# Splitting 512 tokens in 258 and 254 columns in place of 264 and 248 in the seven-product pairs of a float32 decoder trunk

## The reference, cut to what matters

```
D_MODEL, SEQ, D_FF = 1024, 512, 2816
def swiglu(h, w_gate, w_up, w_down):
    return (jax.nn.silu(h @ w_gate) * (h @ w_up)) @ w_down

h = h + 0.5 * swiglu(rmsnorm(h, ffn1_norm[layer]), ffn1_w_gate[layer], ffn1_w_up[layer], ffn1_w_down[layer])
...
h = h + 0.5 * swiglu(rmsnorm(h, ffn2_norm[layer]), ffn2_w_gate[layer], ffn2_w_up[layer], ffn2_w_down[layer])
```

## Time and profile before

| what | value |
|---|---|
| median of 3 runs | 2118.63 us (2118.48 to 2120.15) |
| span of the profiled execution, first to last instruction | 2115.9 us |
| TensorE busy | 2105.4 us, 13030 matmuls |
| of these on L813 to L815 (seven-product pairs) | 5712, which is 68 pairs of 84 |
| VectorE, ScalarE, GpSimd busy | 1306.5, 812.3, 1552.4 us |
| mean granted TensorE clock | 0.999 |

### The profile page before, as it was taken

The page is one execution under the profiler, slowest core; times in us unless marked ns, Lnnn a source line. Parts: engine busy times, 40 slices in busy tenths (PEclk is TensorE's granted clock), DMA queues, the critical chain, the costliest instruction groups (busy, mean ns, idle before and its releaser), DMA issues. The chain is left out here.

```text
span 2115.9 us, 36325 instructions
## 1 busy us (share of the span) xinstructions
PE 2105.4 (100%) x13030; PEld 1856.4 (88%) x13030; DVE 1306.5 (62%) x1949; ACT 812.3 (38%) x1546; POOL 1552.4 (73%) x1390
## 2 busy tenths in 40 slices
PE   9999999999999999999999999999999999999998
PEld 7899988888888899998889998886878888999987
DVE  6876796695444576664376666456872546676533
ACT  5255312034223355541245552134362334555312
POOL 7778897667973778788778887785757557788864
PEclk9999999999999999999999999999999999999999
DMA  5333333223331333333233333332322212333332
GB/s 200 114 120 115 100 95 121 90 80 97 126 104 50 95 101 115 106 101 123 90 99 106 106 110 101 99 100 75 105 89 91 80 61 87 117 101 115 100 95 85
DMA packets 115417, 215.04 MB, mean 102 GB/s; under 512 B 12832, under 2 KB 14400, under 8 KB 115008
## 3 DMA queue, kind: packets, MB, share of 16 engines
q1 hardware_dynamic: 111024, 202.03, 29.9%
q10 hardware_dynamic: 4240, 10.99, 1.5%
HBM read 208.77 MB, written 4.19 MB: 101 GB/s over the span
## 5 line engine op out<-in xcount | busy, mean ns | idle before, releaser
L527 POOL TENSOR_TENSOR w_split<-w_raw,w_split 128x512 fp32r<-128x512 f32 (+1 forms) x486 | 670.3, 1379 | 41.4 <-ACT w_split L1801 1.1
L603 PE MATMUL ps<-x,w_split 128*128 128x512 f32 (+1 forms) x1766 | 682.1, 386 | 0.3 <-DVE tg L2197 0.2
L605 PE MATMUL ps<-x,w_split 128*128 128x512 f32 (+1 forms) x1766 | 674.1, 382 | 0.0
L604 PE MATMUL ps<-x,w_split 128*128 128x512 f32 (+1 forms) x1766 | 673.9, 382 | 0.0
L517 POOL TENSOR_SCALAR w_split<-w_raw 128x512 fp32r<-128x512 f32 x482 | 335.1, 695 | 351.6 <-PE ps L605 336.9
L813 PE MATMUL ps<-x,w_split 128*128 128x264 f32 (+1 forms) x1904 | 535.1, 281 | 1.1 <-DVE ps L2300 1.0
L815 PE MATMUL ps<-x,w_split 128*128 128x264 f32 (+1 forms) x1904 | 535.1, 281 | 0.0
L814 PE MATMUL ps<-x,w_split 128*128 128x264 f32 (+1 forms) x1904 | 533.5, 280 | 0.0
L603 PEld LDWEIGHTS ps<-x,w_split 128*128 128x128 f32 x1766 | 331.8, 188 | 74.0 <-issue 9.4
L605 PEld LDWEIGHTS ps<-x,w_split 128*128 128x128 f32 x1766 | 331.9, 188 | 64.9
L604 PEld LDWEIGHTS ps<-x,w_split 128*128 128x128 f32 x1766 | 332.0, 188 | 64.7 <-issue 1.4
(11 more groups left out here) (342 smaller groups left out, 2476.0 us busy)
## 6 DMA issues: line engine op xcount, KB each, us to landing
w_raw<-in_stream SPq DMA_DIRECT2D x758, 256.0 KB, 2.8
arena<-in_memT ACTq DMA_DIRECT2D x2, 1024.0 KB, 5.8
s_tables<-kv ACTq DMA_DIRECT2D x4, 512.0 KB, 3.0
arena<-s_tables ACTq DMA_DIRECT2D x4, 512.0 KB, 4.4
out<-h ACTq DMA_DIRECT2D x6, 256.0 KB, 2.3
h<-in_xT SPq DMA_DIRECT2D x4, 256.0 KB, 4.8
h<-in_xT SPq DMA_DIRECT2D x2, 512.0 KB, 6.1
w_raw<-in_stream SPq DMA_DIRECT2D x5, 128.0 KB, 5.0
```

The lines of the kernel that those rows point to most:

```text
L527: pool.tensor_tensor(lo, x, hi.bitcast(F32), ALU.subtract).then_inc(split_ready if half else S("half_split"), 1)
L603: pe.matmul(dst, wh, xh, start=start, stop=False)
L604: pe.matmul(dst, wh, xl, start=False, stop=False)
L605: return pe.matmul(dst, wl, xh, start=False, stop=stop)
```

## The change

One constant is changed. Everything that is worked out from it moves with it: the four wide products go from 264 to 258 columns, the three narrow ones from 248 to 254; the copies, joins and token sums change their widths in the same way; `LEAD` goes from 16 to 4; the narrow moving operands begin at column 258, byte 1032 of the row, in place of 264, byte 1056; and the product B11 is written from column 254 of its bank in place of 248.

```
-FIRST_T, SECOND_T = 264, 248
+FIRST_T, SECOND_T = 258, 254
 LEAD = FIRST_T - SECOND_T
```

## The result

The changed kernel takes 2127.03 us (median) against 2118.85 us for the kernel before: the ratio is 1.0031, with a 95% interval of 1.0020 to 1.0042. It is slower, by 8.2 us in the medians. One of the six runs of the changed kernel was disturbed (5424 us) and counts in neither. The profiled execution took 2127.03 us with a span of 2125.2 us, 9.3 us above the span of before. In all runs whose own span is on record the time is 1.8 to 2.5 us above it; the 2.7 us named ahead of the prediction set a median against the span of one execution. By an estimate from these figures that execution took 2117.7 to 2118.4 us, less than the median, so some of the 9.3 us is that, and not the change.

A forecast was written before the change was run, and what follows sets the result against it. TensorE, busy 2105.4 of 2115.9 us, was taken as the bound. Per pair -0.06 + 0.22 = +0.15 us after rounding, over 68 pairs +10.2 us, median 2118.6 to 2128.8 us; own range 2126 to 2134, 8-in-10 range 2112.5 to 2134.

The forecast's parts named there:

- Term 1: Four wide products of a pair, 48 matmuls of 258 in place of 264 columns: 5.76 against 5.82 us, a 0.06 us gain.
- Term 2: Three narrow products of a pair, 36 matmuls of 254 in place of 248 columns: 4.32 against 4.10 us, a 0.22 us loss.
- The 256 row: Profile row of 256-column matmuls, 95 starts in 11.39 us, 119.9 ns each; taken as the price of 254 and 258 columns.
- the forecast's own bounds: Whole change: +7.6 us with straight pieces through the 248, 256 and 264 rows; +15 us if 258 columns kept 121.3 ns.
- The staircase: TensorE's pitch is columns plus a fixed cost of 17 to 24 cycles, rounded up to 16; inferred from 248, 256, 264, 512.
- The straight line: Rival, chance 0.16: pitch grows evenly from 248 to 264 columns, 0.46 ns a column; -2.3 us, no change that shows.
- The lower step: Rival, chance 0.13: 254 columns still take 272 cycles, under 115 ns, while wide products settle at 119.9; -4.4 to -5.8 us.
- The signs that the prediction named beforehand: Changed pair's timeline: every product 1.44 us; T3 at 1.36, 1.39 to 1.40 or 1.52 shows a rival; wide 1.46 refutes.
- The start off the grid: Rival, chance 0.10: narrow operands from byte 1032, no multiple of 16, cost 6.7 ns more per matmul; +27 us, 2145.
- Parts 3 to 5: Joins and copies: 8 ns each at most, covered; token adds 29 ns, 0 to +0.5 us kept; no new TensorE wait.

The follow-up runs named there:

- the second: The changed kernel (258 and 254) run and profiled once more, unchanged, beside the split of 256: 1.0032 (1.0020 to 1.0045) of the kernel before.
- The streams of one width: Trunk left out; TensorE alone streams 48 matmuls for each width and start: from column 0, 254 columns 117.6 ns, 258 119.9, 260 118.7.
- the start at 256: Changed kernel, but TensorE reads the narrow operands from column 256 (byte 1024) in place of 258: 1.0026 (1.0016 to 1.0036) of the kernel before.

## Why the prediction was right, and where its sizes were off

*What bounds the kernel.* Right. TensorE has no new wait, and the even pairs with nothing beside them take the kernel's times.

*The time.* 2128.8 us was predicted, 2127.0 measured; +10.2 us against +8.2, from a pair of 10.07 against 10.02 and 10.05 us. By the even pairs alone it is +6.9 in that profile and +6.7 in the second; part of the nearness of 8.2 to 10.2 is therefore luck. The direction, and the reason for it, that the narrow products lose more than the wide ones win because 254 columns cost far more than 248, hold.

*Term 1, the wide products (48 x 119.9 ns = 5.76 us, a gain of 0.06 us).* They take 5.78 and 5.79 us (2.88 + 1.46 + 1.44, and 2.89 + 1.44 + 1.46), 120.4 and 120.6 ns: a gain of 0.03 to 0.04 us. A stream of 258 has my 119.9; behind narrow products it does not hold it.

*Term 2, the narrow products (36 x 119.9 ns = 4.32 us, a loss of 0.22 us).* This is the term that was mis-sized. They take 4.24 and 4.26 us, 117.8 and 118.3 ns: a loss of 0.14 to 0.16 us. The 256 row was the nearest row and stood for one product of three. The two errors partly cancel, which is why the sum is nearer than its terms. The lower of the forecast's own bounds, straight pieces through the rows of 248, 256 and 264 columns, would have been the better figure: 118.4 and 120.2 ns, a pair of 10.03 us, +7.6 us. The streams of one width give no reason for it, though, since there 260 columns cost less than 258.

*The staircase.* As a rule it fell. It was inferred from four widths; 18 widths and other starts show no grid of 16 cycles (116.7, 117.6, 118.7, 122.3 ns). One of its four supports was not in the rows either: 264 columns outside the pairs had 120.6 ns, which is 289.4 cycles and not 288. Where it was used, at 254 and 258, it said 120 for both; 258 alone has that, 254 alone has 116.7. The even 120 ns and the uneven 264 that I read as a fixed cost near 24 are patterns of a stream, not places on a step. The Trainium skill's line ("TensorE: Matmul & The Clock Gate", Back-to-back issue gap), which the page gives for isolated matmuls, comes to 108.3 ns at 254 columns, and the trace disagrees there too.

*The rivals.* The straight line is refuted by the falling pitches, though for 254 alone its 116.7 ns happens to be the measured one. The lower step is refuted: no stream of 254 is under 116.7 ns, and its limit was 115. The signs that the prediction named beforehand would have misled: T3 at 1.40 us in the first and third block is the straight line's figure, not the forecast's 1.44, and of the wide products B22 is at 1.46, the figure that was to refute the first term. A single product told less than the sum of the seven. The start off the grid is refuted by the stream and by the start at 256. The line rule on 16 bytes ("SBUF — State Buffer", Specifications, in the Trainium skill) does not order what was measured: 254 columns touch 64 lines from each of the three starts tried, and byte 1032 is the cheapest; 248 columns touch 63 lines from columns 258 and 262, and these are the cheapest and the dearest of four starts (113.5 and 117.4 ns).

*Parts 3 to 5.* Joins 8 ns, token adds 25 ns where 29 was worked out, 0.2 us more of waits in the pairs: as predicted.

*What stays open.* What inside TensorE makes the patterns is not settled: a weight load and a moving stream share each pitch, but no run separates them. Nor is it shown what picks 10.05 in place of 10.02.

## What to carry to other kernels

Where TensorE is a plain stream with a weight load for every matmul and some 250 columns, take the price of a width from a stream of whole groups in their own order, alone on the core: it gave the kernel's pair to the nanosecond in most blocks, and within 0.03 us where the kernel took up another pattern (10.05 at 258), while prices of single widths (268: 120.0 ns alone, 124.4 in the pair) and of one part of a change at a time did not add up. Sweep such a width in steps of two before settling it: here 260 and 252 beat 264 and 248 by 0.12% and 258 and 254 by 0.4% with no other edit. The nearest row gave the direction here and missed the narrow pitch by 1.8% (119.9 against 117.8 ns); by the same row 260 and 252 would have been slower too (10.08 us a pair), and they are faster (9.87).

## What the runs showed of the hardware that was not expected

The pitch of three-part float32 matmuls is not monotone in the columns (258: 119.9 ns, 260: 118.7, 262: 122.3, 264: 120.0). It depends on the column at which the moving operand starts (248 columns: 113.5 ns from 258, 117.4 from 262) and not, in the widths tried, on the column written in PSUM. A stream keeps a pattern of several matmuls for long: 254 columns run a whole product at 120 ns behind 258, and 268 columns stay at 124.4 for all later pairs once a narrow product has gone ahead. Full work on VectorE and ScalarE beside it, and on GpSimd by itself, moves the pitch of one width by less than 0.1 ns. Beside a VectorE that never paused, one GpSimd operation on 128 x 512 elements was shown as 175.7 us long; with VectorE done, such operations took 1.2 us.
